# Seven PSUM banks as one pool for the attention stage of a hybrid decoder step

## What is computed

```
def query_block(q0):                                   # 128 queries
    o_c, imp = nsa_cmp_attend(qb, t, kc, vc)           # compressed keys (64 of them)
    ...
    o_s = gathered_attend(qb, kg, vg, ...)             # selected blocks; all 16 fit in the top 16
    o_w = window_attend(qb, t, wb[:, :, 0], wb[:, :, 1], kpos_w)
    return gb[:, :, 0] * o_c + gb[:, :, 1] * o_s + gb[:, :, 2] * o_w

def mem_attend(q, mkv):
    s = jnp.einsum('bqhd,bmhd->bhqm', q, mkv[:, :, 0]) * SCALE
    p = jax.nn.softmax(s.astype(jnp.float32), axis=-1)
    return jnp.einsum('bhqm,bmhd->bqhd', p.astype(mkv.dtype), mkv[:, :, 1])
```

## Time and profile before

| | |
|---|---|
| median of 3 runs | 932.8 us (931.89 to 933.34) |
| profiled execution | 931.09 us |
| its span, first to last instruction | 929.2 us |
| mean granted TensorE clock | 0.999 |
| PE busy | 896.1 us (96%) |
| PEld busy | 811.6 us (87%) |
| DVE busy | 523.1 us (56%) |
| ACT busy | 413.5 us (44%) |
| POOL busy | 288.1 us (31%) |

### The profile page before, as it was taken

The page is one execution under the profiler, slowest core; times in us unless marked ns, Lnnn a source line. Parts: engine busy times, 40 slices in busy tenths (PEclk is TensorE's granted clock), DMA queues, the critical chain, the costliest instruction groups (busy, mean ns, idle before and its releaser), DMA issues.

```text
span 929.2 us, 20479 instructions
## 1 busy us (share of the span) xinstructions
PE 896.1 (96%) x7594; PEld 811.6 (87%) x7594; DVE 523.1 (56%) x1501; ACT 413.5 (44%) x1063; POOL 288.1 (31%) x497
## 2 busy tenths in 40 slices
PE   6999999999999999999999999899999999999997
PEld 6999999999999999999988787778878788878885
DVE  4656332422323365655656787687787867845443
ACT  6443221224444111012466666576666657833221
POOL 0123212222225435535145153226323522610000
PEclk9999999999999999999999999999999999999999
DMA  8564414325240543231859065545804113534331
GB/s 230 164 203 148 142 49 149 117 75 122 67 145 32 137 134 116 78 106 64 222 128 292 4 182 204 157 123 149 221 10 143 46 48 115 177 108 149 129 121 68
DMA packets 85220, 117.91 MB, mean 127 GB/s; under 512 B 12930, under 2 KB 67506, under 8 KB 84546
## 3 DMA queue, kind: packets, MB, share of 16 engines
q1 hardware_dynamic: 71666, 73.12, 27.2%
q0 software_dynamic: 10224, 36.20, 11.8%
q10 hardware_dynamic: 3232, 7.28, 2.1%
HBM read 91.50 MB, written 32.02 MB: 133 GB/s over the span
## 4 chain that ended last, share of the span: by engine, by line
PE 85%; DVE 6%; issue 4%; ACT 3%; DMA 1%; POOL 0%; ACTq 0%; DVEq 0%; SPq 0%; POOLq 0%
PE psum L601 9%; PE psum L602 8%; PE psum L603 8%; PE psum L1892 8%; PE psum L1771 5%; PE psum L1748 4%; PE psum L1913 3%; PE psum L1911 3%; PE psum L1912 3%; PE psum L1749 3%; PE psum L852 2%; PE psum L588 2%; PE psum L854 2%; PE psum L853 2%; PE psum L589 2%
## 5 line engine op out<-in xcount | busy, mean ns | idle before, releaser
L601 PE MATMUL psum<-a_whi,f_xhi 128*128 128x256 f32 (+1 forms) x672 | 194.7, 290 | 1.6 <-DVE f_xlo L1077 1.4
L602 PE MATMUL psum<-a_wlo,f_xhi 128*128 128x256 f32 (+1 forms) x672 | 190.1, 283 | 0.0
L603 PE MATMUL psum<-a_whi,f_xlo 128*128 128x256 f32 (+1 forms) x672 | 189.6, 282 | 0.0
L2001 ACT ACTIVATE p_P<-psum,p_nb 128x640 f32<-128x640 f32 (+7 forms) x224 | 124.3, 561 | 28.7 <-DVE p_nb L2073 20.3
L601 PEld LDWEIGHTS psum<-a_whi,f_xhi 128*128 128x128 f32 x672 | 127.1, 189 | 4.1 <-DVE a_wlo L577 1.8
L602 PEld LDWEIGHTS psum<-a_wlo,f_xhi 128*128 128x128 f32 x672 | 127.4, 190 | 0.0
L603 PEld LDWEIGHTS psum<-a_whi,f_xlo 128*128 128x128 f32 x672 | 127.3, 189 | 0.0
L754 POOL DMA_DIRECT2D h_scratch<-a_hst x93 | 50.9, 549 | 232.6 <-DVE a_hst L1137 119.2
L1771 PE MATMUL psum<-f_ident,p_P 128*128 128x128 f32 x656 | 99.0, 275 | 3.0 <-DVE s_KTw L1951 1.1
L1771 PEld LDWEIGHTS psum<-f_ident,p_P 128*128 128x128 f32 x656 | 76.8, 140 | 9.3 <-DVE s_KTw L1951 1.3
L2073 DVE CUSTOM_DVE_ANT_0 psum<-psum,p_near 128x256 f32<-128x256 f32 (+7 forms) x96 | 64.7, 673 | 34.7 <-PE psum L1749 29.0
(11 more groups left out here) (339 smaller groups left out, 2126.3 us busy)
## 6 DMA issues: line engine op xcount, KB each, us to landing
a_wraw<-in_w_in SPq DMA_DIRECT2D x24, 512.0 KB, 4.3
h_scratch<-a_hst POOLq DMA_DIRECT2D x72, 128.0 KB, 3.6
s_SG<-in_cache_nsa_slc SPq DMA_DIRECT2D x64, 128.0 KB, 3.5
p_qd<-q_scratch SPq DMA_DIRECT2D x16, 384.0 KB, 7.5
a_xraw<-in_x_prompt SPq DMA_DIRECT2D x8, 512.0 KB, 7.0
s_MK<-in_cache_mem SPq DMA_DIRECT2D x8, 512.0 KB, 7.8
s_WG<-in_cache_nsa_win SPq DMA_DIRECT2D x8, 512.0 KB, 4.5
mix_scratch<-p_zt POOLq DMA_DIRECT2D x8, 512.0 KB, 4.0
```

The source lines that it names most:

```text
L601: nc.tensor.matmul(out, hi, wh, start=first, stop=False)
L602: nc.tensor.matmul(out, hi, wl, start=False, stop=False)
L603: return nc.tensor.matmul(out, lo, wh, start=False, stop=last)
L2001: nc.scalar.activation(dst, s_view(s), ACT.Exp, bias=nb[:, g % NNB:g % NNB + 1], scale=1.0 if s[2] == 3 else -1.0, accum_out=ssum[:, par[i ...
```

## The change

The seven banks 0 to 6 become one pool. A table, made in Python when the kernel is built, gives every unit one bank or two neighbouring banks (`score_at`) and every chunk one bank (`chunk_at`). The two heads of a memory unit now lie side by side in one bank. With this, 72 units need two banks and 72 need one. The table is made by `give_banks()`, which walks `p_steps` with a clock of its own for PE, and keeps for each bank the time at which it expects it to be free: a chunk's bank 2000 ns after it was turned, a unit's banks 3000 ns after its scores or 2000 ns after the last chunk of the unit two before it was turned, whichever is later. It takes a bank that is free by then, if there is one: for scores an even pair (or any single bank) below 4 first, for chunks a bank from 4 on first; if none of the preferred ones is free, any that is free; if none at all is free, the one that comes free first. PE then waits, ahead of a unit's scores and ahead of a chunk, for whoever used the bank before, as the table tells (`wait_bank_read`): for a chunk until it was read, for a unit until its exponentials are done. Chunks after the last scores use banks 4 to 6 only, and `project` of the last stage, which writes to banks 0 to 3, waits for the chunks that lay there. The order of the steps, the instructions of the engines and the SBUF buffers stay as they are.

```diff
     def softmaxes(v):
 
         i, l = UNITS[v]
-        base, at = 1024 * ((v + 1) % 2), sm_before[v]
+        base, at = 512 * score_at[v], sm_before[v]
         if l >= 16:
             m = l - 16
-            return [(at + j, 24 + 2 * m + j, 3, 2 * m + j, 0, NM, [(base + 512 * j, NM)], 256 * j) for j in range(2)]
+            return [(at + j, 24 + 2 * m + j, 3, 2 * m + j, 0, NM, [(base + 256 * j, NM)], 256 * j) for j in range(2)]
...
+    def give_banks():
+        free, user = [0.0] * 7, [[] for _ in range(7)]
+        chunk_at, chunk_after, score_after, now, held, turned_at = {}, {}, {}, 0.0, {}, {}
+        last_scores = max(k for k, (what, _) in enumerate(p_steps) if what == "qk")
+        cost = {"sq": 500, "mq": 1000, "mt": 220, "mv": 1000, "sc": 700, "si": 110, "sv": 1700, "o": 330}
+
+        def take(places, fits, who):
+            ready = [p for p in places if max(free[b] for b in p) <= now]
+            best = [p for p in ready if fits(p)] or ready or places
+            p = min(best, key=lambda p: max(free[b] for b in p))
+            after = [u for b in p for u in user[b]]
+            for b in p:
+                user[b] = [who]
+            return p, after
+
+        for k, (what, n) in enumerate(p_steps):
+            if what == "qk":
+                need = banks_needed(n)
+                places = [[(2, 3)], [(0, 1)]][n] if n < 2 else [tuple(range(b, b + need)) for b in range(8 - need)]
+                p, score_after[n] = take(places, lambda p: p[-1] < 4 and (need == 1 or p[0] % 2 == 0), ("scores", n))
+                score_at[n] = p[0]
+                now += sum(2 * max(110, w / 2.19) for _, w, _, _ in score_parts(n))
+                held[n] = p
+                for b in p:
+                    free[b] = max(now + 3000, turned_at.get(n - 2, 0) + 2000)
+            elif what == "t":
+                kind = p_chunks[n]
+                places = [(b,) for b in ((4, 5, 6) if k > last_scores else range(7))]
+                p, chunk_after[n] = take(places, lambda p: p[0] >= 4, ("chunk", n))
+                chunk_at[n] = p[0]
+                now += 110 * len(kind[2]) if kind[0] == "p" else cost.get(kind[0], 440)
+                free[p[0]] = now + 2000
+                if kind[0] == "p":
+                    v = kind[1]
+                    turned_at[v] = now
+                    for b in held.get(v + 2, ()):
+                        if user[b] == [("scores", v + 2)]:
+                            free[b] = max(free[b], now + 2000)
+            elif what == "pv":
+                now += 110 * len(p_chunks[n[0]][2])
+        return chunk_at, chunk_after, score_after
...
+    def wait_bank_read(eng, after):
+
+        wait_chunks_read(eng, [n for who, n in after if who == "chunk"])
+        units = [n for who, n in after if who == "scores"]
+        if units:
+            eng.wait_ge(S("p_exp"), sm_count(max(units)))
...
-            if v >= 2:
-                pe.wait_ge(S("p_exp"), sm_count(v - 2))
+            wait_bank_read(pe, score_after[v])
...
-            if c >= 3:
-                wait_chunk_read(pe, c - 3)
-            o = bank(4 + c % 3)
+            wait_bank_read(pe, chunk_after[c])
+            o = bank(chunk_at[c])
...
                 pe.wait_ge(S("p_exp"), SM * QT)
+                wait_chunks_read(pe, [c for c in range(len(p_chunks)) if chunk_at[c] < 4])
```

More of the change, by code:

```diff
@@ L1360, in build @@
                 [(8, 128), (9, 128), (10, 128), (11, 128)], [(T_NEWS, 64), (T_NEWW, 64), (T_CMP, 64)]]
+    score_at = [0] * len(UNITS)
     def numbers(g):
@@ L1559, in build, with banks_needed @@
     p_chunks, p_steps, p_act = schedule()
+    def banks_needed(v):
+        return len({at // 512 for at, _, _, _ in score_parts(v)})
+    def give_banks():
[37 more added lines that the diff above has]
+        return chunk_at, chunk_after, score_after
@@ L1560, in build @@
+    chunk_at, chunk_after, score_after = give_banks()
     mm_rank = {dj: k + 1 for k, dj in enumerate(n for what, n in p_steps if what == "d")}
@@ L1938, in pt_copy @@
             eng.wait_ge(S("p_pv"), pv_freed[p_index[r - NPT]])
-        copy(PTs[r % NPT][0:w, 0:128 * n], bank(4 + c % 3)[0:w, 0:128 * n]).then_inc(sem, 1)
+        copy(PTs[r % NPT][0:w, 0:128 * n], bank(chunk_at[c])[0:w, 0:128 * n]).then_inc(sem, 1)
     def sample_copy(eng, copy, c, sem):
-        kind, src = p_chunks[c], bank(4 + c % 3)
+        kind, src = p_chunks[c], bank(chunk_at[c])
         eng.wait_ge(S("p_tr"), c + 1)
@@ L1966, in split_src @@
         r = tile_rows(D_ORDER[p_chunks[c][1]])
-        return bank(4 + c % 3).rearrange("p (j c) -> p j c", j=4)[:, :, 0:r]
+        return bank(chunk_at[c]).rearrange("p (j c) -> p j c", j=4)[:, :, 0:r]
     kv_rows = lambda c: hD[0:T, c:c + 256]
@@ L2094, in normalize @@
                 dve.wait_ge(S("p_mix"), n - 1)
-            nc.vector.tensor_tensor(Oi[n % 2][:, 0:n_g, :], bank(4 + c % 3, n_g * HD).rearrange("p (u d) -> p u d", d=HD),
+            nc.vector.tensor_tensor(Oi[n % 2][:, 0:n_g, :], bank(chunk_at[c], n_g * HD).rearrange("p (u d) -> p u d", d=HD),
                                     w.rearrange("p (u o) -> p u o", o=1).to_broadcast([128, n_g, HD]), ALU.mult).then_inc(S("pt_dve"), 1)
@@ L2104, in sample_chunk @@
         def sample_chunk(c):
-            kind, o = p_chunks[c], bank(4 + c % 3)
+            kind, o = p_chunks[c], bank(chunk_at[c])
             dve.wait_ge(S("p_tr"), c + 1)
```

## The result

| | before | after |
|---|---|---|
| median | 933.07 us (931.89 to 933.51, 4 runs) | 923.41 us (922.38 to 925.55, 4 runs) |
| profiled execution | 931.09 us | 923.25 us |
| its span | 929.2 us | 921.4 us |

The ratio is 0.9901, with a 95% interval of 0.9888 to 0.9915: the kernel is 9.7 us faster. The forecast was 924.7 us, 8.1 us faster.

What follows compares the result with a forecast made beforehand. PE, busy in 96% of the span, was taken as the bound. Bank waits of 21.6 us x 0.70 x 0.85 x 2/3, less 0.5, gave 8.1 us: from 932.8 to 924.7 us, range 915.5 to 933.5 us.

Steps and rivals of the forecast that it cites:

- The account of before: Attention stage: PE's waits for a bank's previous user sum to 21.6 us, the most a perfect pool could give.
- Old waits removed: Waits ahead of scores and chunks in the attention stage: 70% of the 21.6 us taken as removable by the pool.
- 636.50: An output chunk waits 1.41 us for DVE's late copy; 0.63 us won, as the following `pv` needs the same copy.
- Where the pool has a bank to spare: Spare banks come from one-bank units; two-bank runs keep the old layout; 64% to 81% of the stall, 70% taken.
- The wait at 568.23: A 0.94 us stall between two-bank units, counted among those for which the pool has no spare bank.
- Wrong guesses of the planner: A bank that the planner calls free nearly always is, since its grace is long in real time; new stalls 0.5 us.
- rival 3: Crossed waits: scores wait for chunks' copies, chunks for other units' exponentials, making the kernel slower, 936.8 us; chance 0.11.
- Moved waits: Some bank waits move to chunks needing the same exponentials, or to products needing the same copies; about 85% can be won.
- two factors: 0.85 for what PE's next steps need anyway, 2/3 for gains kept when PE reaches late DVE or ACT work sooner.
- Rival 2: Waits only move to the data, since loop turn, exponential, turn stays closed; about 931.3 us; chance 0.19.
- Rival 1: The pool wins nearly all, 18.4 us, if DVE and ACT move forward with PE entirely; 914.4 us; chance 0.10.
- The extra semaphore instructions: In PE's queue, up to two more per unit at 51 ns, at most 14.7 us if none were hidden; taken as 0.

Runs made afterwards that it cites:

- the two runs with a true clock: Changed kernel, planner's clock given the trace's step times: 927.6 us with 2000 and 3000 ns kept, 923.3 us with 2900 and 4300 ns.
- the tables from seen times: Changed kernel, planner's times replaced by those its trace saw: 921.7 us; made again from that run's trace: 920.6 us.

## Why the prediction was right, and where it was not

**The account of before** holds. The bound of 21.6 us for all bank waits is 20.2 by the finer count, and the table above shows that these waits are the whole lever.

**Old waits removed.** I took 70% of 21.6, 15.1 us. The two old kinds fell from 20.3 to 4.3 us: 16.0. The size was right, though the reason given for it was not. Single stalls went otherwise than I had split them: at 636.50 I expected 0.63 us won of 1.41 and the rest back at the product. Instead 1.16 us came back at the chunk behind, for the same copy.

**Where the pool has a bank to spare.** This is the step that failed. I wrote that in a run of large units the planner gives "even pairs and banks 4 to 6 in turn, that is, the old layout". It does not. 158 chunks lie below bank 4, 52 units reach above bank 3, and 37 of 72 pairs start at an odd bank. The wait at 568.23, between two-bank units, which I had counted as not helped, is gone, and so is the one at 736.81. That one-bank units feed the pool is right (3 to 5 us lost when 16 of them take two banks), but they feed it everywhere and not only where they stand.

**Wrong guesses of the planner.** I put 0.5 us for new stalls, and the crossed waits are 5.5 us: 4.9 for scores behind copies and 0.6 for chunks behind exponentials. Taken by its words, the term was right: at the 305 choices where the planner held a bank free, all waits together are 0.1 us, as I had argued from the grace. But at the other 192 it held none free and took the one that should come free first, and there stands nearly all of the 9.8 us of bank waits, at 22 choices. By the trace, for about half of that time there was no free bank or pair at all, and for the other half another one came free earlier than the one taken. My sum had no term for these choices, since in the old layout, which I took the rule to give, scores and chunks never share a bank. So the new stalls were too small by a factor of ten, and this follows from the failed step. (The planner's clock adds up to 243 us and not 242, which changes nothing.)

It was rival 3's mechanism, and by the letter its sign came too: I had written that waits for copies in new places of over 5 us would show it, and the two new rows of scores behind copies have 5.1 us. The kernel is faster all the same, because more was removed. The mechanism can be large: with other choices on the same banks it made the kernel 10.8 us slower than before, and with chunks behind exponentials 17.8 us. The grace holds down the part of it that comes from banks called free too early, as the two runs with a true clock show (927.6 us with the short grace, 923.3 with the long one).

**Moved waits.** I expected them at the chunks, by the exponentials, and at the products, by the copies, and both came: 2.3 and 3.0 us, against 0.9 before. I took two factors for what comes back, 0.85 and 2/3, which make 6.5 us of 15.1. Seen are 5.3 - 0.9 = 4.4 us. So the errors partly cancel, and that is luck: I had 5.0 us too few of crossed waits, 0.9 us too little removed, and 2.1 us too much lost to moved waits.

**The sum.** The waits fell by 6.0 us, and the span by 7.8, where I had 8.1. 1.8 us of the span are in neither wait, so that the total came out within 0.3 us is luck as well: the waits alone would have given 6.0. The attention stage accounts for 7.4 us of the 7.8 (335.9 to 328.5), and the stage began 0.5 us earlier (475.5 and 475.0 us). The other 1.4 us of it are probably the waits' own edges. At the median, the weight load of a step that waited begins 0.04 us after the release, while that of a step that didn't wait begins 0.03 us before the end of the load ahead of it. With 56 waits before and 38 after, that is 18 x 0.07 = 1.3 us, an estimate. The medians differ by 1.9 us more than the spans, 9.7 us; this is the profiled execution of before, which lay 2 us below its median, at a granted clock of 0.999, while that of the changed kernel lay at its median.

**The rivals.** Rival 2 (the waits only move to the data) is there as a part: of 16.0 us removed, 4.4 came back that way. In the tables from seen times it becomes the larger part, 6.3 and 7.2 us of data waits beside 6.0 and 5.2 at the banks. Rival 1 (nearly all of it) needs the order of the steps to change, not the table; no run here tried that.

The extra semaphore instructions, taken at 0, show no sign of a cost: 89 units wait for a chunk in the changed kernel, and 100 in the kernel that takes the bank placed longest ago, whose remainder in the last column is that of the others (909.2 us, against 909.9 where only scores are pooled and no unit waits for a chunk).

## What to carry to other kernels

Find out how long each kind of user holds a buffer before pooling them. Here a unit's bank is held more than twice as long as a chunk's; the pool paid with a choice by the expected release, and the same pool with a choice by age alone lost 27 us against it. Look also at what the choice does when nothing is free: nearly all waits that were left stood there. Be careful with half a pool: here the scores kept fixed places, and lending them to chunks in between made the scores wait, and PE with them. In an in-order schedule, count beside the waits that go what the next steps of the same engine need anyway; here a quarter of what the pool removed came back as waits for data, and a third as waits of one kind of user for the other.

## What the runs showed of the hardware that was not expected

Nothing of the hardware itself. Granted clocks were 0.994 to 0.999 in all runs, and small differences between single executions go with them: without the preference, the two executions at 0.999 took 923.1 and 923.4 us, those at 0.996 and 0.997 took 925.8 and 926.0 us. One thing on reading a profile: in one place, 569.79, a wait for two semaphores was put down to the wrong engine by the row of the weight load, and the row of the matmul named the right one.
